# The first two weight units of a two-layer encoder: loaded and split in halves from a second queue, their products interleaved

## The chip, the cores and the metric

The kernel runs on one NeuronCore of one Trainium2 chip. The metric is device time in microseconds for one execution, the median over several runs. Everything (activations, both layers' attention, a dense feed-forward and a routed one with eight experts) is one launch.

## The reference

The input x is 512 rows of 1024 numbers in float32. Two layers follow each other; what concerns the change is the first step of the first one.

```python
h = rmsnorm(x, norm_mix[layer])      # x * rsqrt(mean(x*x)) * gain
...
proj = h @ w_in                      # 1024 x 4352: keys, queries, values, gates
...
merged = gates[:, :, 0] * (ya @ w_branch_a) + gates[:, :, 1] * (yb @ w_branch_b)
x = x + merged @ w_out
...
x = x + swiglu(...)  # layer 0;  x = x + moe_swiglu(...)  # layer 1, top 2 of 8 experts
```

## The kernel before

**Number format.** [...] A product is three matmuls: high weights by high activations, high weights by low activations, low weights by high activations.

**Units.** Weights come in units of 128 x 1024 floats (512 KB): eight tiles of 128 x 128, that is, 128 columns of a weight matrix over all 1024 rows of its input. `raw` holds four units as they land, `w_hi` and `w_lo` two split ones. For each unit ScalarE writes `w_hi` (L796, `split_hi`), VectorE writes `w_lo` (L1139, `split_lo`), TensorE makes 8 x 3 matmuls of 128x512, and it adds one to `unit_done`. Since there are two split buffers, ScalarE's split of unit n waits for `unit_done` to reach n - 1: the split of unit 2 waits for the products of unit 0.

**The input and its norm.** `xs` holds x transposed, in eight tiles k of 128 x 512 (256 KB each). ScalarE multiplies a tile by the gain and writes its high part `h_hi` (L849), VectorE the low part `h_lo` (L1164). The norm's factor is not known yet: the products of the first units run on the unscaled h, and the results are multiplied by `rms_inv` when they are evicted (L1178). Meanwhile ScalarE squares the tiles of x (L806) and VectorE adds them into `norm` (L1156, L1159). TensorE sums over the partitions (`mean_square`, L1686), ScalarE takes the root (L814), VectorE the reciprocal (L1169), which it places on a diagonal (L1173), TensorE spreads it over the partitions (`spread_rinv`, L1692), and ScalarE copies it out (`rms_inv`, L854).

**Queues.** All engines run their own list in program order; the order of the work is written by hand.
- SyncE issues the loads: gains, x0, unit 0, x1, unit 1, x2 to x7, units 2 and 3, and small tensors. A later unit n waits for `lo_ready` to reach n - 3.
- ScalarE: a warm-up of the root (its table load), x0, unit 0, x1, unit 1, x2 to x7, squares of x0 and x1, the split of unit 2 (behind the wait for unit 0's products), six more squares, the split of unit 3, the root, `rms_inv`. It issues no DMA.
- VectorE follows it with the low parts and the sums, in the same order.
- TensorE: 13 matmuls on an idle tile (`keep_warm`, L1662), then the 16 tile products of units 0 and 1 (`first_product`, L1736, L1738, L1741) in the order of `FIRST_PRODUCTS`: of unit 0 two tiles, of unit 1 two, then the six others of unit 0, then the six others of unit 1. Then unit 2 (`unit_ready` is a wait for its low part) with the mean before its sixth tile, unit 3 with the spread after its first tile, and unit after unit from there.

The matmuls of units 2 and up are L1655 to L1657.

Of the kernel before, what the change touches and what calls it, by code (L numbers as in the profile page):

```python
# [5 lines left out]
F32 = mybir.dt.float32  # L6
# [4 lines left out]
ALU = mybir.AluOpType  # L11
# [5 lines left out]
T = 512  # L17
# [51 lines left out]
def build_kernel(nc, xT, g_mix, w_in, b_gate, rel_ext, sinks, w_a, w_b, w_out, g_ffn, w_gu, w_down, w_router,  # L69
                 moe_gu, moe_down, g_ffn_row, g_final_row, out):  # L70
    ctx = ExitStack()
    with ctx:
# [3 lines left out]
        def sem(name):  # L76
            return ctx.enter_context(nc.semaphore(name))
# [189 lines left out]
        y0_done = sem("y0_done")  # L267
        last_rows_ready, last_hi, last_lo, placed, kept = (sem(n) for n in ("last_rows_ready", "last_hi", "last_lo", "placed", "kept"))
# [131 lines left out]
        def term(m, which):  # L400
# [7 lines left out]
        FIRST_PRODUCTS = ((0, 0), (0, 1), (1, 0), (1, 1), (0, 2), (0, 3), (0, 4), (0, 5), (0, 6), (0, 7),  # L408
                          (1, 2), (1, 3), (1, 4), (1, 5), (1, 6), (1, 7))
# [19 lines left out]
        def _(sp):  # L429
# [15 lines left out]

            sp.dma_start(gains[:, 0:DEPTH, :], g_mix).then_inc(gains_in, 16)
            load_x(0)
            load(0, w_in[0, 0])
            load_x(1)
            load(1, w_in[0, 1])  # L450
            for k in range(2, KD):
                load_x(k)
# [336 lines left out]
        def _(act_):  # L789
# [65 lines left out]

            A.wait_ge(basics, 1)
            warm_root()
            for k in range(2):
                h_split_hi(k)
                split_hi(k)  # L860
            for k in range(2, KD):
                h_split_hi(k)
# [272 lines left out]
        def _(V):  # L1135
# [54 lines left out]
            for k in range(2):  # L1190
                h_split_lo(k)
                split_lo(k)
            for k in range(2, KD):
                h_split_lo(k)
# [453 lines left out]
        def _(E):  # L1648
# [81 lines left out]
            def first_product(u, k):  # L1730

                (wh, wl), bank = split_of(u, k * P, (k + 1) * P), unit_bank(u)
                if k == 0:
                    E.wait_ge(hi_ready, u + 1)
                E.wait_ge(h_hi_ready, k + 1)
                E.matmul(ps[:, bank, :], wh, h_hi[:, k, :], start=k == 0, stop=False)  # L1736
                E.wait_ge(h_lo_ready, k + 1)
                E.matmul(ps[:, bank, :], wh, h_lo[:, k, :], start=False, stop=False)  # L1738
                if k == 0:
                    E.wait_ge(lo_ready, u + 1)  # L1740
                mm = E.matmul(ps[:, bank, :], wl, h_hi[:, k, :], start=False, stop=k == KD - 1)  # L1741
                if k == KD - 1:
                    mm.then_inc(unit_done, 1)

            E.wait_ge(basics, 3)
            keep_warm(13)
# [405 lines left out]
```

## Time and profile before

| | us |
|---|---|
| median of 3 runs | 1596.53 |
| lowest, highest | 1594.66, 1598.08 |
| the profiled execution's own time | 1595.05 |
| its span, from the first to the last instruction | 1593.2 |
| TensorE busy in it | 1572.4 |
| VectorE busy | 1012.4 |
| ScalarE busy | 842.6 |

Times in the rows below count from the start of the span. The opening, from the first instruction to unit 5, is the first 46 us. A row of the timeline gives a start and a length, and in brackets how long the engine had been idle before it and what it waited for. Lengths of matmuls are modelled; from one start to the next is the measured pace.

### The profile page before, as it was taken

Reading aid. Unit: us, or ns where it says so; the run is one execution under the profiler, and the core shown is the slowest. Engines: PE = TensorE matmul, PEld = TensorE weight load, DVE = VectorE, ACT = ScalarE, POOL = GpSimd, SP = SyncE. Lnnn points to the kernel's source line nnn. Section 1 sums busy time; section 2 is a strip of 40 time slices with the busy share of each in tenths; the row PEclk is TensorE's granted clock in tenths of the full one; section 3 lists DMA queues with packets and bytes.
Section 4 is the critical chain, followed back from the end, with each engine's and each line's share of the span. In section 5 each row is a group of like instructions: output and inputs, shape, how many; then the busy total and the mean of one; then the engine's idle time right before and its main releaser. Section 6 shows DMA issues by size and latency. Waiting matters only on the chain.

```text
span 1593.2 us, 22686 instructions
## 1 busy us (share of the span) xinstructions
PE 1572.4 (99%) x7620; PEld 1312.9 (82%) x7621; DVE 1012.4 (64%) x1699; ACT 842.6 (53%) x1321; POOL 236.7 (15%) x290
## 2 busy tenths in 40 slices
PE   9999999999999999999999999999999999999997
PEld 6788888788888888888888887778888888888886
DVE  6657765654444443346567666666666998887577
ACT  5436764343232332234357663566666888885564
POOL 0204563000000000002015660010101001110000
PEclk9999999999999999999999999999999999999999
DMA  7632222344454333335422123448767999996673
GB/s 221 193 100 68 68 64 70 96 142 137 141 149 129 93 91 100 91 103 149 114 70 78 54 67 93 159 164 292 242 221 242 376 382 376 382 373 216 205 245 131
DMA packets 90067, 266.37 MB, mean 167 GB/s; under 512 B 12594, under 2 KB 22834, under 8 KB 89969
## 3 DMA queue, kind: packets, MB, share of 16 engines
q1 hardware_dynamic: 82864, 248.59, 47.6%
q0 software_dynamic: 7104, 16.52, 3.3%
q8 instruction: 55, 0.90, 0.2%
q14 instruction: 44, 0.35, 0.1%
HBM read 243.63 MB, written 20.22 MB: 166 GB/s over the span
## 4 chain that ended last, share of the span: by engine, by line
PE 93%; DVE 4%; DMA 1%; issue 1%; ACT 1%; SPq 0%; POOL 0%; DVEq 0%; ACTq 0%; POOLq 0%
PE ps L1655 18%; PE ps L1656 17%; PE ps L1657 17%; PE ps L1992 8%; PE ps L1994 8%; PE ps L1993 8%; PE ps L1991 4%; PE ps L1990 4%; PE ps L1826 2%; PE ps L1859 1%; PE ps L1839 1%; PE ps L1858 1%; PE ps L1838 1%; PE ps L2001 1%; DVE w_lo L1139 1%; PE ps L1973 1%
## 5 line engine op out<-in xcount | busy, mean ns | idle before, releaser
L1655 PE MATMUL ps<-h_hi,w_hi 128*128 128x512 f32 x880 | 350.8, 399 | 1.6 <-DVE w_lo L1139 1.6
L796 ACT ACTIVATE w_hi<-raw 128x1024 fp32r<-128x1024 f32 (+1 forms) x168 | 175.9, 1047 | 327.1 <-PE ps L1657 323.7
L1656 PE MATMUL ps<-h_lo,w_hi 128*128 128x512 f32 x880 | 343.7, 391 | 0.0
L1657 PE MATMUL ps<-h_hi,w_lo 128*128 128x512 f32 x880 | 343.5, 390 | 0.0
L1139 DVE TENSOR_TENSOR w_lo<-raw,w_hi 128x1024 fp32r<-128x1024 f32 x136 | 164.4, 1209 | 136.2 <-ACT w_hi L796 136.0
L1144 DVE TENSOR_TENSOR m_lo<-m_raw,m_hi 128x1024 fp32r<-128x1024 f32 x144 | 168.4, 1192 | 68.9 <-ACT m_hi L836 61.0
L1657 PEld LDWEIGHTS ps<-h_hi,w_lo 128*128 128x128 f32 x880 | 165.2, 188 | 35.7
L1655 PEld LDWEIGHTS ps<-h_hi,w_hi 128*128 128x128 f32 x880 | 165.6, 188 | 27.7 <-issue 2.7
L1656 PEld LDWEIGHTS ps<-h_lo,w_hi 128*128 128x128 f32 x880 | 165.9, 189 | 25.5 <-issue 0.7
L836 ACT ACTIVATE m_hi<-m_raw 128x1024 fp32r<-128x1024 f32 x144 | 145.9, 1032 | 62.0 <-PE ps L1991 49.3
L1992 PE MATMUL ps<-m_hi,xt_hi 128*128 128x512 f32 (+1 forms) x320 | 120.3, 376 | 0.6 <-DVE xt_both L1148 0.6
L1144 DVE TENSOR_TENSOR m_lo<-h_rows,m_hi 128x1024 fp32r<-128x1024 f32 (+1 forms) x96 | 102.0, 1087 | 29.1 <-ACT m_hi L836 29.1
L1994 PE MATMUL ps<-m_hi,xt_lo 128*128 128x512 f32 (+1 forms) x320 | 119.4, 373 | 0.0
L1993 PE MATMUL ps<-m_lo,xt_hi 128*128 128x512 f32 (+1 forms) x320 | 119.3, 373 | 0.0
L836 ACT ACTIVATE m_hi<-h_rows 128x1024 fp32r<-128x1024 f32 (+1 forms) x96 | 90.1, 950 | 51.1 <-PE ps L1991 39.2
L595 POOL TENSOR_TENSOR w_lo<-raw,w_hi 128x512 fp32r<-128x512 f32 x64 | 82.5, 1291 | 52.0 <-DVE probs L1274 51.1
L607 POOL DMA_DIRECT2D norm<-rel_rows x16 | 9.7, 604 | 540.1 <-issue 465.7
L723 POOL DMA_INDIRECT xg<-h_dram,lists x18 | 24.1, 1337 | 372.7 <-PE ps L1973 296.1
L919 ACT ACTIVATE pT_hi<-ps 128x256 fp32r<-128x256 f32 (+3 forms) x128 | 50.5, 395 | 40.1 <-PE ps L1826 36.8
L1992 PEld LDWEIGHTS ps<-m_hi,xt_hi 128*128 128x128 f32 x320 | 60.1, 188 | 10.2 <-issue 0.8
L1655 PE MATMUL ps<-a_hi,w_hi 128*128 128x512 f32 x176 | 68.5, 389 | 0.0
L1656 PE MATMUL ps<-a_lo,w_hi 128*128 128x512 f32 x176 | 68.5, 389 | 0.0
(304 smaller groups left out, 3210.9 us busy)
## 6 DMA issues: line engine op xcount, KB each, us to landing
m_raw<-moe_g SPq DMA_DIRECT2D x88, 512.0 KB, 5.3
raw<-w_in SPq DMA_DIRECT2D x68, 512.0 KB, 3.6
m_raw<-moe_down SPq DMA_DIRECT2D x56, 512.0 KB, 6.1
raw<-w_gu SPq DMA_DIRECT2D x44, 512.0 KB, 3.7
h_rows<-moe_g SPq DMA_DIRECT2D x32, 512.0 KB
h_rows<-moe_g SPq DMA_DIRECT2D x32, 384.0 KB
h_rows<-moe_down SPq DMA_DIRECT2D x24, 512.0 KB
m_raw<-moe_g SPq DMA_DIRECT2D x24, 384.0 KB, 5.4
```

The costliest lines, as they stand in the source:

```text
L595: ins = pool.tensor_tensor(lo, raw[:, n % RAW, c0:c1], hi.bitcast(F32), ALU.subtract)
L796: A.activation(split_of(n, 0, cols)[0], raw[:, n % RAW, 0:cols], ACT.Copy).then_inc(hi_ready, 1)
L836: A.activation(hi_of(u)[:, 0:cols], raw_of(u)[:, 0:cols], ACT.Copy).then_inc(m_hi_ready, 1)
L1139: V.tensor_tensor(lo, raw[:, n % RAW, 0:cols], hi.bitcast(F32), ALU.subtract).then_inc(lo_ready, 1)
L1144: V.tensor_tensor(lo_part(u)[:, 0:cols], raw_of(u)[:, 0:cols], hi_of(u)[:, 0:cols].bitcast(F32), ALU.subtract).then_inc(m_lo_ready, 1)
L1655: E.matmul(ps[:, bank, :], wh, hi, start=first, stop=False)
L1656: E.matmul(ps[:, bank, :], wh, lo, start=False, stop=False)
L1657: return E.matmul(ps[:, bank, :], wl, hi, start=False, stop=final)
L1990: E.matmul(out, both[:, x, :], wh, start=start, stop=False)
L1992: E.matmul(out, hi[:, x, :], wh, start=start, stop=False)
L1993: E.matmul(out, hi[:, x, :], wl, start=False, stop=False)
L1994: return E.matmul(out, lo[:, x, :], wh, start=False, stop=stop)
```

## The change

**Loads.** The halves of units 0 and 1 (four tiles each, 256 KB) are loaded by four DMAs that ScalarE issues: the first halves of both before its table load, the second halves after the warm-up of the root. SyncE no longer loads units 0 and 1; it issues x0 first, then the gains, x1 to x7, units 2 and 3.

**Splits.** ScalarE and VectorE split units 0 and 1 in halves, in between the tiles of x. First halves have semaphores of their own (`early_raw`, `early_hi`, `early_lo`); the second halves use those of whole units.

**Products.** `FIRST_PRODUCTS` goes tile by tile: tile 0 of unit 0, tile 0 of unit 1, tile 1 of unit 0, and so on. TensorE waits for a half before tiles 0 and 4. The matmuls on the idle tile are 9 instead of 13.

```diff
--- before.py
+++ after.py
@@ -265,6 +265,7 @@
         rel_copied = [sem("rel_copied0"), sem("rel_copied1")]
         zero_sent, mix_open, premixed = sem("zero_sent"), sem("mix_open"), sem("premixed")
         y0_done = sem("y0_done")
+        early_raw, early_hi, early_lo = [sem("early_raw0"), sem("early_raw1")], sem("early_hi"), sem("early_lo")
         last_rows_ready, last_hi, last_lo, placed, kept = (sem(n) for n in ("last_rows_ready", "last_hi", "last_lo", "placed", "kept"))
         y_back = [sem(f"y_back{m}") for m in range(2 * TT)]
         mixed, mix_step, sq_ready, root_ready, inv_ready, scaled, act_out, dve_out = sem("mixed"), sem("mix_step"), sem("sq_ready"), sem("root_ready"), sem("inv_ready"), sem("scaled"), sem("act_out"), sem("dve_out")
@@ -405,8 +406,12 @@
 
         GATES_AT = {4 * g: g for g in range(N_GATE)}
 
-        FIRST_PRODUCTS = ((0, 0), (0, 1), (1, 0), (1, 1), (0, 2), (0, 3), (0, 4), (0, 5), (0, 6), (0, 7),
-                          (1, 2), (1, 3), (1, 4), (1, 5), (1, 6), (1, 7))
+        FIRST_PRODUCTS = [(u, k) for k in range(KD) for u in range(2)]
+        def first_half(n, half):
+            return slice(half * T, (half + 1) * T)
+
+        def split_half(n, half):
+            return split_of(n, half * T, (half + 1) * T)
 
         def halves(u):
 
@@ -443,12 +448,9 @@
             def load_x(k):
                 sp.dma_start(xs[:, k, :], xT[:, k, :]).then_inc(x_in[k], 16)
 
+            load_x(0)
             sp.dma_start(gains[:, 0:DEPTH, :], g_mix).then_inc(gains_in, 16)
-            load_x(0)
-            load(0, w_in[0, 0])
-            load_x(1)
-            load(1, w_in[0, 1])
-            for k in range(2, KD):
+            for k in range(1, KD):
                 load_x(k)
             load(2, w_in[0, 2])
             load(3, w_in[0, 3])
@@ -853,13 +855,32 @@
                 A.wait_ge(rinv_spread, j + 1)
                 A.activation(rms_inv[:], ps[:, SUM_BANK, :], ACT.Copy).then_inc(rms_ready, 1)
 
+            def load_half(n, half):
+                A.dma_start(raw[:, n, first_half(n, half)], w_in[0, n][:, first_half(n, half)]
+                            ).then_inc(raw_full[n] if half else early_raw[n], 16)
+
+            def split_hi_half(n, half):
+                A.wait_ge(raw_full[n] if half else early_raw[n], 16)
+                A.activation(split_half(n, half)[0], raw[:, n, first_half(n, half)], ACT.Copy).then_inc(hi_ready if half else early_hi, 1)
+
+            load_half(0, 0)
+            load_half(1, 0)
             A.wait_ge(basics, 1)
             warm_root()
-            for k in range(2):
-                h_split_hi(k)
-                split_hi(k)
-            for k in range(2, KD):
-                h_split_hi(k)
+            load_half(0, 1)
+            load_half(1, 1)
+            h_split_hi(0)
+            split_hi_half(0, 0)
+            h_split_hi(1)
+            split_hi_half(1, 0)
+            h_split_hi(2)
+            h_split_hi(3)
+            split_hi_half(0, 1)
+            h_split_hi(4)
+            split_hi_half(1, 1)
+            h_split_hi(5)
+            h_split_hi(6)
+            h_split_hi(7)
             square(0, 0)
             square(1, 1)
             split_hi(2)
@@ -1187,11 +1208,23 @@
                                        op1=ALU.max).then_inc(consts, 1)
                 V.wait_ge(consts, 3)
 
-            for k in range(2):
-                h_split_lo(k)
-                split_lo(k)
-            for k in range(2, KD):
-                h_split_lo(k)
+            def split_lo_half(n, half):
+                V.wait_ge(hi_ready if half else early_hi, n + 1)
+                hi, lo = split_half(n, half)
+                V.tensor_tensor(lo, raw[:, n, first_half(n, half)], hi.bitcast(F32), ALU.subtract).then_inc(lo_ready if half else early_lo, 1)
+
+            h_split_lo(0)
+            split_lo_half(0, 0)
+            h_split_lo(1)
+            split_lo_half(1, 0)
+            h_split_lo(2)
+            h_split_lo(3)
+            split_lo_half(0, 1)
+            h_split_lo(4)
+            split_lo_half(1, 1)
+            h_split_lo(5)
+            h_split_lo(6)
+            h_split_lo(7)
             sum_squares(0, 0)
             sum_squares(1, 1)
             split_lo(2)
@@ -1730,20 +1763,20 @@
             def first_product(u, k):
 
                 (wh, wl), bank = split_of(u, k * P, (k + 1) * P), unit_bank(u)
-                if k == 0:
-                    E.wait_ge(hi_ready, u + 1)
+                if k % 4 == 0:
+                    E.wait_ge(hi_ready if k else early_hi, u + 1)
                 E.wait_ge(h_hi_ready, k + 1)
                 E.matmul(ps[:, bank, :], wh, h_hi[:, k, :], start=k == 0, stop=False)
                 E.wait_ge(h_lo_ready, k + 1)
                 E.matmul(ps[:, bank, :], wh, h_lo[:, k, :], start=False, stop=False)
-                if k == 0:
-                    E.wait_ge(lo_ready, u + 1)
+                if k % 4 == 0:
+                    E.wait_ge(lo_ready if k else early_lo, u + 1)
                 mm = E.matmul(ps[:, bank, :], wl, h_hi[:, k, :], start=False, stop=k == KD - 1)
                 if k == KD - 1:
                     mm.then_inc(unit_done, 1)
 
             E.wait_ge(basics, 3)
-            keep_warm(13)
+            keep_warm(9)
             for layer in range(DEPTH):
                 n0 = MIX_START[layer]
                 norm_i = 2 * layer

```

What stands on ScalarE at its start before (`warm` is the warm-up of the root, `raw` and `w_hi` belong to weight units, `xs` and `h_hi` to the tiles of x):

```order
L810 ACT_TABLE_LOAD
L810 ACTIVATE warm<-eps 128x1 [waits basics]
L849 ACTIVATE h_hi<-xs,gains 128x512 [waits gains_in,x_in0]
L796 ACTIVATE w_hi<-raw 128x1024 [waits raw_full0]
L849 ACTIVATE h_hi<-xs,gains 128x512 [waits x_in1]
L796 ACTIVATE w_hi<-raw 128x1024 [waits raw_full1]
L849 ACTIVATE h_hi<-xs,gains 128x512 [waits x_in2]
L849 ACTIVATE h_hi<-xs,gains 128x512 [waits x_in3]
L849 ACTIVATE h_hi<-xs,gains 128x512 [waits x_in4]
```

and after the change:

```order
L859 DMA raw<-w_in 128x512 x2
L812 ACT_TABLE_LOAD
L812 ACTIVATE warm<-eps 128x1 [waits basics]
L859 DMA raw<-w_in 128x512 x2
L851 ACTIVATE h_hi<-xs,gains 128x512 [waits gains_in,x_in0]
L864 ACTIVATE w_hi<-raw 128x512 [waits early_raw0]
L851 ACTIVATE h_hi<-xs,gains 128x512 [waits x_in1]
L864 ACTIVATE w_hi<-raw 128x512 [waits early_raw1]
L851 ACTIVATE h_hi<-xs,gains 128x512 [waits x_in2]
L851 ACTIVATE h_hi<-xs,gains 128x512 [waits x_in3]
L864 ACTIVATE w_hi<-raw 128x512 [waits raw_full0]
L851 ACTIVATE h_hi<-xs,gains 128x512 [waits x_in4]
```

Four DMAs stand ahead of the first tile of x, and each split of a whole unit has become two of half its width, the second ones behind x3 and x4.

TensorE's first products before, where each group of three matmuls is a tile (the first two groups are unit 0, the third is unit 1):

```order
L1736 MATMUL ps<-h_hi,w_hi 128x512 [waits h_hi_ready,hi_ready]
L1738 MATMUL ps<-h_lo,w_hi 128x512 [waits h_lo_ready]
L1741 MATMUL ps<-h_hi,w_lo 128x512 [waits lo_ready]
L1736 MATMUL ps<-h_hi,w_hi 128x512 [waits h_hi_ready]
L1738 MATMUL ps<-h_lo,w_hi 128x512 [waits h_lo_ready]
L1741 MATMUL ps<-h_hi,w_lo 128x512
L1736 MATMUL ps<-h_hi,w_hi 128x512 [waits h_hi_ready,hi_ready]
L1738 MATMUL ps<-h_lo,w_hi 128x512 [waits h_lo_ready]
L1741 MATMUL ps<-h_hi,w_lo 128x512 [waits lo_ready]
```

and after the change (the first group is unit 0, the second unit 1, the third unit 0 again):

```order
L1769 MATMUL ps<-h_hi,w_hi 128x512 [waits h_hi_ready,early_hi]
L1771 MATMUL ps<-h_lo,w_hi 128x512 [waits h_lo_ready]
L1774 MATMUL ps<-h_hi,w_lo 128x512 [waits early_lo]
L1769 MATMUL ps<-h_hi,w_hi 128x512 [waits h_hi_ready,early_hi]
L1771 MATMUL ps<-h_lo,w_hi 128x512 [waits h_lo_ready]
L1774 MATMUL ps<-h_hi,w_lo 128x512 [waits early_lo]
L1769 MATMUL ps<-h_hi,w_hi 128x512 [waits h_hi_ready]
L1771 MATMUL ps<-h_lo,w_hi 128x512 [waits h_lo_ready]
L1774 MATMUL ps<-h_hi,w_lo 128x512
```

Unit 1's first tile has moved from the third to the second place, and the waits for a whole unit have become waits for its first half.

ScalarE again, behind the last tile of x, before (L806 are squares, L796 the splits of units 2 and 3):

```order
L806 ACTIVATE ps<-xs 128x512 [waits x_in0]
L806 ACTIVATE ps<-xs 128x512 [waits x_in1]
L796 ACTIVATE w_hi<-raw 128x1024 [waits unit_done,raw_full2]
L806 ACTIVATE ps<-xs 128x512 [waits summed,x_in2]
L806 ACTIVATE ps<-xs 128x512 [waits summed,x_in3]
L806 ACTIVATE ps<-xs 128x512 [waits summed,x_in4]
L806 ACTIVATE ps<-xs 128x512 [waits summed,x_in5]
```

and after:

```order
L808 ACTIVATE ps<-xs 128x512 [waits x_in0]
L808 ACTIVATE ps<-xs 128x512 [waits x_in1]
L798 ACTIVATE w_hi<-raw 128x1024 [waits unit_done,raw_full2]
L808 ACTIVATE ps<-xs 128x512 [waits summed,x_in2]
L808 ACTIVATE ps<-xs 128x512 [waits summed,x_in3]
L808 ACTIVATE ps<-xs 128x512 [waits summed,x_in4]
L808 ACTIVATE ps<-xs 128x512 [waits summed,x_in5]
```

Nothing moved here but the line numbers: the split of unit 2 waits for unit 0's products, and the squares of x2 to x7 stand behind it.

## Rows read from the trace of the kernel before

**Rows 1.** the page of the whole kernel, its parts 1 and 4

```profile
PE 1572.4 (99%) x7620; PEld 1312.9 (82%) x7621; DVE 1012.4 (64%) x1699; ACT 842.6 (53%) x1321; POOL 236.7 (15%) x290
...
PE 93%; DVE 4%; DMA 1%; issue 1%; ACT 1%; SPq 0%; POOL 0%; DVEq 0%; ACTq 0%; POOLq 0%
```

**Rows 2.** stretches: length, busy us (instructions) of each engine, PEclk, DMA share, GB/s

```profile
0.00:7.00 7.00, 5.21 (x13) 1.82 (x14) 0.77 (x2) 3.24 (x6) 2.32 (x15) 1.00 0.64 211
7.00:12.00 5.00, 3.94 (x15) 2.11 (x14) 4.27 (x5) 3.95 (x7) 0.00 (x0) 1.00 1.02 351
```

**Rows 3.** who waited for whom, first 60 us: us in total, times, longest

```profile
PE ps L1741 <- DVE w_lo L1139: 1.1, 2, 0.5
```

**Rows 4.** timeline from 0: start us, us, engine, line, operation, tiles, count, [idle <-releaser]

```profile
0.83 1.28 ACT L810 ACT_TABLE_LOAD   x1 [0.68 <-PEq L2144]
...
0.83 0.39 SPq L446 DMA_DIRECT2D gains<-g_mix  x1
...
1.27 0.43 SPq L444 DMA_DIRECT2D xs<-xT  x1
...
1.79 5.43 PE L1662 MATMUL ps<-idle 128*128 128x512 bf16 x13 [1.79 <-POOL ident L560]
...
2.12 0.20 ACT L810 ACTIVATE warm<-eps 128x1 f32<-128x1 f32 x1
...
39.93 0.57 POOL L580 DMA_DIRECT2D k_hi<-k_hi  x1 [0.38 <-POOL norm L613]
```

**Rows 5.** timeline near 1053 us, TensorE

```profile
1053.34 1.24 PE L1662 MATMUL ps<-idle 128*128 128x512 bf16 x5
```

**Rows 6.** timeline, ScalarE and VectorE, 4 to 14 us

```profile
4.47 0.72 ACT L849 ACTIVATE h_hi<-xs,gains 128x512 fp32r<-128x512 f32 x1 [2.15 <-DMA xs<-xT]
...
5.23 0.75 DVE L1164 SCALAR_TENSOR_TENSOR h_lo<-xs,gains,h_hi 128x512 fp32r<-128x512 f32 x1 [5.09 <-ACT h_hi L849]
...
5.98 1.06 ACT L796 ACTIVATE w_hi<-raw 128x1024 fp32r<-128x1024 f32 x1 [0.79 <-DMA raw<-w_in]
...
8.53 1.06 ACT L796 ACTIVATE w_hi<-raw 128x1024 fp32r<-128x1024 f32 x1 [0.88 <-DMA raw<-w_in]
...
11.60 2.03 ACT L849 ACTIVATE h_hi<-xs,gains 128x512 fp32r<-128x512 f32 x3 [0.17 <-DMA xs<-xT]
```

**Rows 7.** timeline, TensorE's first products, 7 to 16 us

```profile
7.09 0.50 PE L1736 MATMUL ps<-h_hi,w_hi 128*128 128x512 f32 x1
...
10.91 0.50 PE L1741 MATMUL ps<-h_hi,w_lo 128*128 128x512 f32 x1 [0.53 <-DVE w_lo L1139]
...
11.24 0.40 PE L1736 MATMUL ps<-h_hi,w_hi 128*128 128x512 f32 x1
...
15.79 0.39 PE L1741 MATMUL ps<-h_hi,w_lo 128*128 128x512 f32 x1
```

**Rows 8.** timeline, three engines, 13 to 29 us

```profile
16.28 1.06 ACT L796 ACTIVATE w_hi<-raw 128x1024 fp32r<-128x1024 f32 x1 [1.64 <-PE ps L1741]
...
17.37 1.23 DVE L1139 TENSOR_TENSOR w_lo<-raw,w_hi 128x1024 fp32r<-128x1024 f32 x1 [1.15 <-ACT w_hi L796]
...
18.52 4.64 DVE L1159 TENSOR_TENSOR norm<-norm,ps 128x512 f32<-128x512 f32 x6
...
20.10 0.39 PE L1655 MATMUL ps<-h_hi,w_hi 128*128 128x512 f32 x1
...
23.50 0.95 PE L1686 MATMUL ps<-mean_of,norm 128*128 128x1 f32 x8
...
24.99 0.69 DVE L1173 TENSOR_TENSOR norm<-ident,rinv 128x512 f32<-128x512 f32 x1
...
27.12 1.02 PE L1692 MATMUL ps<-norm,ones 128*128 128x512 f32 x2
28.18 0.60 ACT L854 ACTIVATE rms_inv<-ps 128x512 f32<-128x512 f32 x1 [3.43 <-PE ps L1692]
```

**Rows 9.** timeline, TensorE, its only start after an idle time in 40 to 46 us

```profile
45.38 0.47 PE L1655 MATMUL ps<-h_hi,w_hi 128*128 128x512 f32 x1 [1.56 <-DVE w_lo L1139]
```

## The prediction

> **What bounds the kernel now.** I read the page first. TensorE is busy for 1572.4 of 1593.2 us and makes 93% of the chain that ended last [rows 1], so time comes and goes only where TensorE is held up. The change touches the opening alone, so the next view is the list of waits there. TensorE waited 1.1 us for the low halves of the first two units (L1741) [rows 3], and ScalarE 1.64 us, before it splits unit 2, for TensorE to finish unit 0 [rows 8]. That second wait becomes the important one.
>
> Then the timeline. The first product starts at 7.09; the products run without a break only from the third product of unit 1's first tile, at 10.91 (10.91 to 11.24 is 0.33, a start after an idle time), and from 11.24 to 15.79 twenty starts lie 4.55 us apart, so **0.2275 us per product** [rows 7]. The 48 first products end, and unit 2 begins, at 20.10 [rows 8]. By then three other things have happened: unit 0's last product started at 15.79 [rows 7], ScalarE split unit 2 from 16.28, VectorE took the low half at 17.37 (1.23 us) and then added six squares in 4.64 us, until 23.16 [rows 8]. TensorE reached the mean (L1686) at 23.50, only 0.34 us after the last addition. So two chains run nearly side by side from 16.28 to 23.50: TensorE's products, and ScalarE and VectorE behind the end of **unit 0**. Behind the mean come VectorE's diagonal (24.99 to 25.68), TensorE's spread of the root in program order (27.12), and the evictions that wait for it (28.18) [rows 8]. The evictions pace what follows, for at 45.38 TensorE has stood still 1.56 us for VectorE's w_lo [rows 9]; after that I found no tie to absolute time. A shift of the mean therefore moves the rest of the kernel by as much.
>
> **The opening, step by step.** In blocks of 256 KB (a tile of x, or half a unit), the old queue delivers its 1st at 4.47, 3rd at 5.98, 6th at 8.53 and 10th at 11.60 [rows 6]: some 0.75 to 0.85 us a block. The first x tile is now issued at 0.83 instead of 1.27, as the gains change places with it [rows 4]: 0.44 us earlier. If x0 and unit 0's first half share the engines evenly, both are there when two blocks are, (4.47 + 5.98)/2 - 0.44 = 4.8; x1 and unit 1's first half at 5.98 + 0.85 - 0.44 = 6.4; x2 and unit 0's second half at 8.1; x3 and unit 1's second half (8th block, 8.53 + 1.54 - 0.44) at 9.6; x5 at 11.2. The total to x7 is the same twelve blocks. Without sharing x0 would land at 4.47 - 0.44 = 4.03; that is the lower end. The trace of before has one queue only, so the even share is my choice, on the ground that the DMA engines were full from 7 us on, at 351 GB/s [rows 2], and the bytes are the same. The Trainium skill (DMA: Bandwidth & Descriptors, section Issuing engines are not separate DMA queues) says that transfers started by different engines run on the same 16 DMA engines and interleave, so that the second queue saves issue time and gains no bandwidth; by that rule x0 comes at 4.8 rather than at 4.03, and the sum below is nearer to its +1.5 than to its lower end of +0.7. No run shown yet tells.
>
> ScalarE now issues four DMAs. No DMA of ScalarE is in the trace: SyncE takes 0.39 to 0.43, GpSimd 0.57 [rows 4]. With 0.45 each, two DMAs, the table load of 1.28 and two DMAs end at 0.83 + 0.9 + 1.28 + 0.2 + 0.9 = 4.1 (0.2 for the warm root [rows 4]); at 0.57 each it is 4.6. Either ends before x0 is there, so I cost them at nothing; the cover is 0.2 to 0.7 us.
>
> ScalarE's split of a tile of x takes 0.7 (0.72; three take 2.03), and VectorE's 0.75 [rows 6]. A split of half a unit I take as 0.6 on ScalarE (0.60 for the copy of rms_inv, of that size, and 1.06 for a whole unit) and 0.65 on VectorE (1.23 a whole one) [rows 6, 8]. So ScalarE: x0 4.8 to 5.5, unit 0's half to 6.1, x1 6.4 to 7.1, unit 1's half 7.15 to 7.75. VectorE: x0 5.5 to 6.25, unit 0's half to 6.9, x1 7.15 to 7.9, unit 1's half 7.9 to **8.55**. Product (0, 0) can start at 6.1, and the third product of (1, 0), number 6 of 48, at 8.6. From there all is ready in time: VectorE ends x2 at 9.6, x3 at 11.1, x4 at 12.5, unit 1's second half at 13.15 and x7 near 15.5, while pairs of tiles take 6 x 0.2275 = 1.36 us and the fifth starts at 8.95 + 3 x 1.36 = 13.0, its use of unit 1's half at 14.1, and the last pair at 17.1. The first products end at 8.95 + 42 x 0.2275 = **18.5, which is 1.6 us earlier** than 20.10. Nine warm-ups instead of thirteen (5.43/13 = 0.42 us each [rows 4]) end near 5.6, before the 6.1 at which TensorE is first wanted, and cost nothing by themselves.
>
> **What takes it back.** Unit 0 now ends three products before unit 1, not eighteen. Its last is number 45, at 8.95 + 38 x 0.2275 = 17.6. Before, 0.49 us lay between that product's start and ScalarE's split of unit 2 (15.79 to 16.28), so the split starts at 18.05, **1.77 us later** than before. Everything in that row of the queue follows: low half of unit 2 at 18.05 + 1.09 + 1.23 = 20.4 (TensorE idles 1.9 us after 18.5), last sum at 23.16 + 1.77 = 24.93. TensorE comes to the mean 15 products later, at 20.4 + 3.4 = 23.8, waits over 1 us more, and starts it at 25.0. The shift is 1.77 - 0.34 + 0.05 = **+1.5 us**. ScalarE's other work behind that wait (six squares, the split of unit 3) moves with it; unit 3, whose low half follows the last sum by 0.1 + 1.23, is ready at 26.3, and is wanted at 25.0 + 0.95 + 9 x 0.2275 = 28.0. The spread comes at 27.12 + 1.5, the evictions too, and the start at 45.38 becomes 46.9. The loads of units 2 and 3 and the later ones keep their order and have microseconds to spare.
>
> The profiled execution took 1595.05 (span 1593.2 and 1.85 around it), the median of the three runs is 1596.53. Sum: 1595.05 + 1.5 = 1596.55 against the profiled one, and **1598.0** against the median. Bounds of the sum: with the landings of unit 1 at 5.98 and ScalarE's splits of half of 1.06, number 6 starts at 7.8 and the shift is +0.7; with half a microsecond on each of the two landings it waits for, it starts at 9.6, the shift +2.5.
>
> **Rivals.** (a) *The clock comes up late: slower.* The thirteen warm-ups took 0.42 us each, five later ones 1.24/5 = 0.25 [rows 4, 5]: at first the clock is at its lower level, 1.2 GHz, though the column of granted clock reads 1.00 there [rows 2], and TensorE had worked without a break since 1.79 when it rose. Now the unbroken stretch ends at 5.6, with gaps up to 6.1, 6.9, 7.8 and 8.6. If the clock is still low at 8.6, and stays so as long as the warm-ups ran at it here, the products up to 14.0 run at 0.42 and lose 5.4 x (1 - 0.2275/0.42) = 2.5 us: 1.5 + 2.5 = +4.0, 1600.5. It decides if the first products start over 0.34 us apart. For it speaks the shorter warm-up; against, that TensorE is still at work for over half of 5.6 to 8.6. The Trainium skill (TensorE: Matmul & The Clock Gate, section What's actually happening) says that the throttled state is the default and activity releases it; the rows agree, but don't show what the gaps do.
> (b) *ScalarE's issues are slow, or its transfers late: slower.* At 1.2 us each instead of 0.45 its first split starts at 7.1, 2.3 late, and the shift is +3.8, 1600.3. Against it stand the rows of the two other engines.
> (c) *The 1.6 us are kept.* If unit 2 and the sums of squares were in time, 1596.53 - 1.6 = 1594.9. This needs ScalarE not to be held by unit 0; its queue has unit 2's split behind that very wait, before six of eight squares, so I give it little.
> (d) *The change does nothing:* products as late as before (20.10) through landings 1.6 us later than mine give the late split without the gain: +3.1, 1599.6.
>
> **Numbers.** 0.2% is 3.2 us, about what a measurement of this kernel tells from no change. The forecast (+0.7 to +2.5) has 0.66, (a) 0.15, (b) 0.06, (c) 0.06, (d) 0.07. Slower by over 3.2 us: (a), (b), and a part of (d) and of the forecast with scatter: 0.22. Faster by as much: 0.03, for only scatter beyond (c) gets there. The same: 0.75. Range: 1596.53 + 0.7 less the 1.9 by which the lowest run lies below the median gives 1595.3; the top takes in (a) and (b) with half a microsecond, 1601.0.
>
> **What would show it.** Number 6 of the first products near 8.6 and their end near 18.5; ScalarE idle some 2.5 us or more before it splits unit 2 near 18.0; TensorE idle 1.9 us before unit 2 (on VectorE's w_lo) and 1.2 before the mean (on norm), neither of which is there now; the mean near 25.0, the spread near 28.6. Wrong it would be if the mean came before 23.5, if products up to 14 were 0.42 apart, or if the 1.5 us were taken up in a later wait.

## The result, and the profile after it

The changed kernel takes **1600.37 us** (median of 11 executions, 1598.55 to 1602.92) against 1596.16 us for the kernel before (11 executions, 1594.66 to 1598.47). The ratio is 1.0030, with a 95% interval of 1.0022 to 1.0038: about 4 us slower, and slower by more than 0.2%. The profiled execution took 1599.41 us, its span is 1597.7, 4.5 more than before. Some executions are slower than any profile here shows: seven of the 49 of kernels with the interleaved order have a mean granted clock of 0.994 and took 1601.1 to 1604.0 us, none of the 154 listed of kernels with the old order is below 0.995, and no trace shows where in them the clock was low.

The page, its parts 1 and 4, against [rows 1]:

```profile
span 1597.7 us, 22686 instructions
...
PE 1573.3 (98%) x7616; PEld 1313.8 (82%) x7617; DVE 1011.1 (63%) x1701; ACT 842.8 (53%) x1323; POOL 236.5 (15%) x290
...
PE 91%; DVE 5%; issue 2%; ACT 1%; DMA 1%; DVEq 0%; ACTq 0%; POOL 0%; SPq 0%; POOLq 0%
```

TensorE's busy time grew by 0.9 us only, and the span by 4.5: TensorE stands still more. The timeline shows where, first the issues of the opening (SPq is SyncE's queue, ACTq ScalarE's), then TensorE up to its thirteenth product, with VectorE's low half of unit 1 that the sixth waits for, against [rows 4, 7] (start us, us, engine, line, operation, tiles, count, idle time before it):

```profile
0.83 0.39 SPq L449 DMA_DIRECT2D xs<-xT  x1
0.83 0.90 ACTq L859 DMA_DIRECT2D raw<-w_in  x2
1.27 0.43 SPq L452 DMA_DIRECT2D gains<-g_mix  x1
...
1.83 0.87 ACTq L859 DMA_DIRECT2D raw<-w_in  x2
...
1.79 3.82 PE L1695 MATMUL ps<-idle 128*128 128x512 bf16 x9 [1.79 <-POOL ident L562]
...
6.97 0.51 PE L1769 MATMUL ps<-h_hi,w_hi 128*128 128x512 f32 x1 [1.37 <-ACT w_hi L864]
...
8.58 0.72 PE L1769 MATMUL ps<-h_hi,w_hi 128*128 128x512 f32 x1 [0.24 <-ACT w_hi L864]
8.71 0.69 DVE L1214 TENSOR_TENSOR w_lo<-raw,w_hi 128x512 fp32r<-128x512 f32 x1
9.10 0.63 PE L1771 MATMUL ps<-h_lo,w_hi 128*128 128x512 f32 x1
9.53 0.72 PE L1774 MATMUL ps<-h_hi,w_lo 128*128 128x512 f32 x1
10.04 0.63 PE L1769 MATMUL ps<-h_hi,w_hi 128*128 128x512 f32 x1
...
12.15 0.39 PE L1774 MATMUL ps<-h_hi,w_lo 128*128 128x512 f32 x1
12.38 0.40 PE L1769 MATMUL ps<-h_hi,w_hi 128*128 128x512 f32 x1
```

then the splits of the first two tiles of x, and the stretch behind unit 0, against [rows 6, 8, 9]:

```profile
5.68 0.72 ACT L851 ACTIVATE h_hi<-xs,gains 128x512 fp32r<-128x512 f32 x1 [2.42 <-DMA gains<-g_mix]
...
7.28 0.72 ACT L851 ACTIVATE h_hi<-xs,gains 128x512 fp32r<-128x512 f32 x1 [0.36 <-DMA xs<-xT]
...
19.67 0.39 PE L1774 MATMUL ps<-h_hi,w_lo 128*128 128x512 f32 x1
...
20.16 1.06 ACT L798 ACTIVATE w_hi<-raw 128x1024 fp32r<-128x1024 f32 x1 [5.17 <-PE ps L1774]
...
21.25 1.22 DVE L1160 TENSOR_TENSOR w_lo<-raw,w_hi 128x1024 fp32r<-128x1024 f32 x1 [4.71 <-ACT w_hi L798]
...
22.39 4.64 DVE L1180 TENSOR_TENSOR norm<-norm,ps 128x512 f32<-128x512 f32 x6
22.52 0.50 PE L1688 MATMUL ps<-h_hi,w_hi 128*128 128x512 f32 x1 [1.79 <-DVE w_lo L1160]
...
27.08 1.05 PE L1719 MATMUL ps<-mean_of,norm 128*128 128x1 f32 x8 [0.86 <-DVE norm L1180]
...
28.68 0.69 DVE L1194 TENSOR_TENSOR norm<-ident,rinv 128x512 f32<-128x512 f32 x1
...
30.84 1.02 PE L1725 MATMUL ps<-norm,ones 128*128 128x512 f32 x2
...
31.90 0.60 ACT L856 ACTIVATE rms_inv<-ps 128x512 f32<-128x512 f32 x1 [3.46 <-PE ps L1725]
...
49.09 0.47 PE L1688 MATMUL ps<-h_hi,w_hi 128*128 128x512 f32 x1 [1.55 <-DVE w_lo L1160]
```

Unit 0's last product starts at 19.67 instead of 15.79. ScalarE stood idle for 5.17 us before it could split unit 2 (1.64 before), at 20.16 instead of 16.28. Behind that, TensorE idles 1.79 us for unit 2's low half and 0.86 us for the sums, two waits that were not there. The mean starts at 27.08 (23.50), the copy of rms_inv at 31.90 (28.18): **3.72 us later**. TensorE's start after an idle time is at 49.09 (45.38), with the same 1.55 us of idle time before it, and nothing takes the shift up for 1000 us: the five matmuls on the idle tile that stood at 1053.34 [rows 5] are at

```profile
1057.14 1.24 PE L1695 MATMUL ps<-idle 128*128 128x512 bf16 x5
```

3.80 us later. The issues of the last stores still start 3.7 us later (1588.38 against 1584.70, and 1589.96 against 1586.26). The remaining 0.8 us of the span arises in those stores and their landings; no run ties it to the change.

### The profile page after: what moved, and what is told of

The parts are those of the page before. It is cut to its first block, busy times and chain, and to the rows that moved or that the text cites. A ratio compares the mean times of both kernels' runs of the same rounds, so it can differ in the third digit from the quotient of the medians.

```text
span 1597.7 us, 22686 instructions
## 1 busy us (share of the span) xinstructions
PE 1573.3 (98%) x7616; PEld 1313.8 (82%) x7617; DVE 1011.1 (63%) x1701; ACT 842.8 (53%) x1323; POOL 236.5 (15%) x290
## 4 chain that ended last, share of the span: by engine, by line
PE 91%; DVE 5%; issue 2%; ACT 1%; DMA 1%; DVEq 0%; ACTq 0%; POOL 0%; SPq 0%; POOLq 0%
PE ps L1688 18%; PE ps L1689 17%; PE ps L1690 17%; PE ps L2025 7%; PE ps L2027 7%; PE ps L2026 7%; PE ps L2024 4%; PE ps L2023 4%; PE ps L1859 2%; PE ps L1892 1%; PE ps L1872 1%; PE ps L1891 1%; PE ps L1871 1%; PE ps L2034 1%; PE ps L2006 1%
## 5 line engine op out<-in xcount | busy, mean ns | idle before, releaser
L798 ACT ACTIVATE w_hi<-raw 128x1024 fp32r<-128x1024 f32 x166 | 173.8, 1047 | 328.9 <-PE ps L1690 323.6
L1160 DVE TENSOR_TENSOR w_lo<-raw,w_hi 128x1024 fp32r<-128x1024 f32 (+1 forms) x134 | 161.9, 1208 | 138.0 <-ACT w_hi L798 137.9
L1690 PE MATMUL ps<-a_hi,w_lo 128*128 128x512 f32 x176 | 68.5, 389 | 0.0
```

The lines of the kernel that those rows point to most:

```text
L798: A.activation(split_of(n, 0, cols)[0], raw[:, n % RAW, 0:cols], ACT.Copy).then_inc(hi_ready, 1)
L1160: V.tensor_tensor(lo, raw[:, n % RAW, 0:cols], hi.bitcast(F32), ALU.subtract).then_inc(lo_ready, 1)
L1690: return E.matmul(ps[:, bank, :], wl, hi, start=False, stop=final)
```

## The experiments

Each kernel computes all that the reference asks for. "Split" is the start of the split of unit 2, "copy" that of rms_inv, "restart" TensorE's start after its idle time near 45 us; ratios are to executions of the kernel before on the same chip.

| kernel | split | copy | restart | ratio, interval |
|---|---|---|---|---|
| before | 16.28 | 28.18 | 45.38 | 1 |
| the change | 20.16 | 31.90 | 49.09 | 1.0030, 1.0022 to 1.0038 |
| before, new order alone | 20.10 | 31.82 | 49.03 | 1.0041, 1.0027 to 1.0055 |
| change, old order | 16.13 | 28.02 | 45.21 | 1.0002, 0.9993 to 1.0012 |
| change, 13 warm-ups | 19.36 | 31.10 | 48.29 | 1.0027, 1.0016 to 1.0037 |
| change, gains first | 21.67 | 33.41 | 50.60 | 1.0039, 1.0025 to 1.0052 |
| change, squares first | 20.18 | 30.74 | 47.93 | 1.0023, 1.0013 to 1.0033 |
| change, one queue, 13 warm-ups | 18.79 | 30.54 | 47.73 | 1.0016, 1.0007 to 1.0025 |
| before, 9 warm-ups | 17.87 | 29.77 | 46.96 | 1.0002, 0.9993 to 1.0011 |
| before, mean sooner | 15.69 | 26.23 | 43.70 | 0.9992, 0.9983 to 1.0001 |
| the same again | 15.94 | 26.48 | 43.95 | 0.9994, 0.9986 to 1.0003 |
| change, mean sooner | 16.78 | 27.07 | 44.64 | 0.9999, 0.9990 to 1.0008 |
| before, mean sooner, x0 first | 16.28 | 26.82 | 44.28 | 0.9995, 0.9986 to 1.0004 |

In the first six rows, and wherever the order behind the split is untouched, the copy follows the split by 11.7 to 11.9 us: one number carries the whole opening. Split, copy and restart are of one profiled execution each; ratios whose intervals overlap don't tell two kernels apart.

### The order of the products alone

```diff
 # kernel before
-        FIRST_PRODUCTS = ((0, 0), (0, 1), (1, 0), (1, 1), (0, 2), (0, 3), (0, 4), (0, 5), (0, 6), (0, 7),
-                          (1, 2), (1, 3), (1, 4), (1, 5), (1, 6), (1, 7))
+        FIRST_PRODUCTS = [(u, k) for k in range(KD) for u in range(2)]
```

> The kernel before with the interleaved order of the first products and nothing else (whole loads, whole splits, 13 warm-ups). Theory (unit 0 ends late and holds the split of unit 2 and six squares): the sixth product stays near 10.9, unit 0's last product starts near 19.9 instead of 15.79, ScalarE splits unit 2 near 20.35, and the copy of rms_inv starts near 32.0 instead of 28.18; time +3.8 us against the kernel before. Rival (the order is harmless, the loss is in clock and landings): the copy stays within 0.7 us of 28.18, the time within 1 us.

The timeline of this kernel, ScalarE at unit 2 and TensorE behind it:

```profile
20.10 1.06 ACT L795 ACTIVATE w_hi<-raw 128x1024 fp32r<-128x1024 f32 x1 [5.75 <-PE ps L1740]
...
22.47 0.50 PE L1654 MATMUL ps<-h_hi,w_hi 128*128 128x512 f32 x1 [1.79 <-DVE w_lo L1138]
...
27.03 1.05 PE L1685 MATMUL ps<-mean_of,norm 128*128 128x1 f32 x8 [0.86 <-DVE norm L1158]
...
31.82 0.60 ACT L853 ACTIVATE rms_inv<-ps 128x512 f32<-128x512 f32 x1 [3.44 <-PE ps L1691]
```

The whole pattern of the change is there without its loads, its halves or its shorter warm-up: ScalarE's 5.75 us of idle time, TensorE's 1.79 and 0.86. The copy is 3.64 us late, where 3.8 were expected, and the time is up by 0.41%, 0.27% at the least. The rival is out. The 0.41% are 6.5 us, more than the copy explains: of only five executions two took 1603.08 and 1604.0 us; the medians are 4.5 us apart.

### The change with the old order

```diff
 # changed kernel
-        FIRST_PRODUCTS = [(u, k) for k in range(KD) for u in range(2)]
+        FIRST_PRODUCTS = ((0, 0), (0, 1), (1, 0), (1, 1), (0, 2), (0, 3), (0, 4), (0, 5), (0, 6), (0, 7),
+                          (1, 2), (1, 3), (1, 4), (1, 5), (1, 6), (1, 7))
```

> The changed kernel with the old order of the first products (unit 0 ends eighteen products before unit 1), halves and second queue kept. Theory: the split of unit 2 falls to 16 to 16.8 from 20.16, the copy of rms_inv to 28 to 28.6, time within 0.5 us of the kernel before although its loads are as in the change. Rival (halves and queue are what costs): the copy stays above 30 and the time 3 us or more above the kernel before.

```profile
1.79 4.02 PE L1696 MATMUL ps<-idle 128*128 128x512 bf16 x9 [1.79 <-POOL ident L563]
...
16.13 1.06 ACT L799 ACTIVATE w_hi<-raw 128x1024 fp32r<-128x1024 f32 x1 [1.30 <-PE ps L1775]
...
28.02 0.60 ACT L857 ACTIVATE rms_inv<-ps 128x512 f32<-128x512 f32 x1 [3.43 <-PE ps L1726]
```

Split at 16.13, copy at 28.02, ratio 1.0002. The two runs mirror each other: the order by itself gives the loss, and taking it back removes it with the loads, the halves and nine warm-ups all kept. What these bring or cost together is below what the ratio resolves (0.1% to either side, some 1.5 us).

### Thirteen warm-ups, and nine in the kernel before

```diff
 # changed kernel
-            keep_warm(9)
+            keep_warm(13)
```

```diff
 # kernel before
-            keep_warm(13)
+            keep_warm(9)
```

> The changed kernel with 13 warm-ups instead of 9. Theory (nine products between 8.6 and 12.1 ran 0.43 us apart because the clock fell): all first products 0.23 apart, the split of unit 2 near 18.9 instead of 20.16, the copy of rms_inv near 30.5 instead of 31.9, time 1.4 us below the changed kernel, still some 2.5 above the kernel before. Rival (the warm-ups don't matter): copy at 31.9, or later by the 0.2 us by which the warm-ups outlast the first split.

> The kernel before with 9 warm-ups instead of 13. Theory (the shorter warm-up costs only while products run low behind it, and in the order of before TensorE is waiting for loads until about 10.9 anyway): some first products 0.43 apart, the copy of rms_inv within 0.8 us of 28.2, time +0 to +1 us. Rival (the nine warm-ups are a large part of the change's 4 us): the copy at 29.5 or later, time +1.5 us or more.

First the stretch from 9 to 12.5 us in the changed kernel, then in the one with thirteen warm-ups (busy us and instructions of PE, PEld, DVE, ACT, POOL; then granted clock, DMA share, GB/s):

```profile
9.00:12.50 3.50, 3.50 (x10) 2.48 (x10) 3.02 (x6) 3.38 (x6) 0.00 (x0) 0.56 1.03 366
```

```profile
9.00:12.50 3.50, 3.34 (x13) 2.48 (x14) 3.41 (x6) 3.33 (x6) 0.00 (x0) 1.00 1.05 367
```

In the profiled execution of the change the granted clock was 0.56 in this stretch: for most of it at the lower level, 1.2 GHz. It had been up before: the first two products start 0.35 apart (6.97, 7.32), and the granted clock reads 1.00 from 7 to 8 us, 0.84 from 8 to 9 and 0.50 from 9 to 12; before it fell TensorE had stood idle for 1.37 and 0.24 us. The starts are 0.43 apart from 9.10 to 11.75 (but for one of 0.51) and 0.23 from 12.15 on. With thirteen warm-ups the granted clock is 1.00 and 13 products start, not 10. The split came at 19.36 instead of 20.16, 0.8 us sooner although x1 was split 0.45 us later (7.73 against 7.28). So the slow products behind the short warm-up cost this execution over a microsecond. The copy came at 31.10, not at the 30.5 expected, because x1 was late. The times don't show the 1.4 us that were expected: 1.0027 against 1.0030, with intervals that overlap.

The other kernel shows the same in the old order. Its profile has nine warm-ups and then every first product up to 13.94 at the slow pace; the next starts 0.25 later:

```profile
7.39 0.79 PE L1736 MATMUL ps<-h_hi,w_hi 128*128 128x512 f32 x1 [1.58 <-ACT w_hi L796]
7.99 0.63 PE L1738 MATMUL ps<-h_lo,w_hi 128*128 128x512 f32 x1
...
12.23 0.63 PE L1738 MATMUL ps<-h_lo,w_hi 128*128 128x512 f32 x1
12.66 0.63 PE L1741 MATMUL ps<-h_hi,w_lo 128*128 128x512 f32 x1
...
17.87 1.06 ACT L796 ACTIVATE w_hi<-raw 128x1024 fp32r<-128x1024 f32 x1 [3.34 <-PE ps L1741]
...
29.77 0.60 ACT L854 ACTIVATE rms_inv<-ps 128x512 f32<-128x512 f32 x1 [3.43 <-PE ps L1692]
```

There the copy is 1.6 us late, as the rival had it, yet the ratio over eleven executions is 1.0002. Its interval, 0.9993 to 1.0011, is -1.1 to +1.8 us and leaves room for both, so the runs don't decide between them. When the clock rises differs from one execution to the next: with identical code up to there, thirteen warm-ups took 5.43 us before, 5.73 with the new order alone and 4.48 with the mean sooner. The five profiles with nine warm-ups all have products 0.43 apart behind them, up to 10.6 us (change, old order) at the least and to 13.9 at the most; in none of the eight with thirteen does the slow pace last beyond 8 us. A profile gives the price of the slow pace in one execution; that most executions pay less of it would fit the times, but isn't shown.

### The gains, and one queue instead of two

```diff
 # changed kernel, SyncE: gains first
-            load_x(0)
             sp.dma_start(gains[:, 0:DEPTH, :], g_mix).then_inc(gains_in, 16)
-            for k in range(1, KD):
+            for k in range(KD):
                 load_x(k)
```

```diff
 # changed kernel with 13 warm-ups: SyncE issues the half units, ScalarE none
             load_x(0)
             sp.dma_start(gains[:, 0:DEPTH, :], g_mix).then_inc(gains_in, 16)
-            for k in range(1, KD):
-                load_x(k)
+            load_half(0, 0)
+            load_x(1)
+            load_half(1, 0)
+            load_x(2)
+            load_x(3)
+            load_half(0, 1)
+            load_x(4)
+            load_half(1, 1)
+            for k in range(5, KD):
+                load_x(k)
```

> The changed kernel with the gains issued before x0 again. Theory (x0's split waited for the gains, which landed behind x0 and the half unit): x0's split starts at 4.8 to 5.1 instead of 5.68, the first product near 6.3 instead of 6.97; the mean and the copy of rms_inv gain 0.5 to 0.9 us if the clock stays up and less if it falls. Rival (the landing of x0 itself is late because two queues share the engines): x0's split still at 5.5 or later.

> The change with 13 warm-ups and with its half units issued by SyncE between the tiles of x (x0, gains, unit 0's half, x1, unit 1's half, x2, x3, half, x4, half, x5 to x7), none by ScalarE. Theory (two queues share the engines, so x0 and x1 land late): x0's split starts at 4.0 to 4.6 instead of 5.7, x1's before 6.5 instead of 7.3 to 7.7, and the sixth product starts near 8.5 instead of 9.9; the copy of rms_inv 1 us or more before that of the two-queue kernel with 13 warm-ups (31.10). Rival (one queue delivers as late, the second is harmless): x0 at 5 or later, the copy within 0.4 us of 31.1.

Where the split of x0 had waited for the gains (5.68), with the gains first it waits for x0 itself, and with one queue it starts at 3.85; the kernels in this order:

```profile
5.61 0.72 ACT L850 ACTIVATE h_hi<-xs,gains 128x512 fp32r<-128x512 f32 x1 [2.35 <-DMA xs<-xT]
```

```profile
3.85 0.72 ACT L863 ACTIVATE h_hi<-xs,gains 128x512 fp32r<-128x512 f32 x1 [1.52 <-DMA gains<-g_mix]
...
6.64 0.72 ACT L863 ACTIVATE h_hi<-xs,gains 128x512 fp32r<-128x512 f32 x1 [0.78 <-DMA xs<-xT]
...
8.61 0.51 PE L1773 MATMUL ps<-h_hi,w_hi 128*128 128x512 f32 x1 [0.28 <-ACT w_hi L872]
```

The times from issue to landing take this apart. In the change x0, issued at 0.83, landed 4.2 us later, at 5.0; the gains, issued behind it at 1.27, landed at 5.6 and held the split. With the gains first these landed at 2.9, but x0, now issued at 1.27, took 4.3 us and landed at 5.6 too: the rival's number, and nothing won. With one queue x0, issued at 0.83 again, took 2.7 us and landed at 3.5, the gains at 3.8. The other kernels agree: with x0 first it took 3.5 to 4.3 us beside the half units of ScalarE's queue (four kernels) and 2.7 or 2.8 without (two). From one queue the split starts at 3.85, below the 4.03 that I had given as the lower end, and x1's at 6.64 instead of 7.28 to 7.73. The sixth product starts at 9.33 instead of 9.89, not at the 8.5 expected, because unit 1's half is split at 7.92 only. The copy comes 0.56 us sooner than with two queues (30.54 against 31.10), between theory (1 or more) and rival (0.4); the ratios, 1.0016 and 1.0027, have intervals that overlap. By the Trainium skill (DMA: Bandwidth & Descriptors, section Issuing engines are not separate DMA queues) both queues run on the same engines and interleave; x0's 4.2 us to its landing against 2.7 agree with that. What doesn't fit a plain reading is that the one-queue kernel moved less from 5 to 9 us, 265 GB/s:

```profile
5.00:9.00 4.00, 3.72 (x11) 1.76 (x9) 2.21 (x4) 2.30 (x4) 0.00 (x0) 1.00 0.84 265
```

against 385 in the change and 354 in the kernel before (the row of the same stretch). One execution each; I leave the cause open.

The kernel with the gains first also had the latest split of all, 21.67, and its copy came 1.5 us later than the change's where 0.5 to 0.9 sooner had been expected. Most of that is x1: it landed at 8.5 instead of 7.2, was split at 8.54, and the sixth product started at 10.85 instead of 9.53. The products ran 0.43 apart up to 13.86, which adds 0.2 us to what the change lost to the clock. That the order of the gains delays x1 isn't shown: the last kernel of the changed loads below has the gains first as well, and splits x1 at 7.50.

### The squares ahead of the split

```diff
 # changed kernel, ScalarE; VectorE likewise
-            split_hi(2)
             for k in range(2, KD):
                 square(k, k)
+            split_hi(2)
```

> The changed kernel with all eight squares (ScalarE) and their sums (VectorE) ahead of the split of unit 2, which still waits for unit 0. Theory (the shift has two parts, the late low half of unit 2 and behind it the late sums): TensorE's idle time before unit 2 stays near 1.8 us, the wait of 0.86 us before the mean is gone, so the copy of rms_inv comes 0.9 us nearer to ScalarE's split of unit 2 (10.8 us after its start instead of 11.74), and the time falls by 0.9. Rival (the sums don't matter, the split alone does): the distance stays 11.7.

```profile
22.53 0.50 PE L1688 MATMUL ps<-h_hi,w_hi 128*128 128x512 f32 x1 [2.22 <-DVE w_lo L1160]
...
26.06 0.95 PE L1719 MATMUL ps<-mean_of,norm 128*128 128x1 f32 x8
...
30.74 0.60 ACT L856 ACTIVATE rms_inv<-ps 128x512 f32<-128x512 f32 x1 [3.43 <-PE ps L1725]
```

The idle time before the mean is gone, as said, and the copy follows the split by 10.56 us instead of 11.74 (10.8 expected). TensorE's idle time before unit 2 has grown to 2.22 us, for another reason: here unit 0's last product starts at 19.24, but ScalarE is busy with its last square (from 19.64, 0.60 us), so the squares and no longer unit 0 hold the split, by some 0.45 us. Both parts of the loss are thus seen apart in the profile: about 1 us by the sums, the rest by unit 2's split. The time forecast, 0.9 us less than the change, is neither shown nor refuted: 1.0023 against 1.0030, with intervals that overlap.

### A version that doesn't lose: the mean sooner

In the kernel before ScalarE idled 1.64 us before the split of unit 2, TensorE did the mean only before its sixth tile, and the spread only behind unit 3's first. This edit uses all three, in the kernel before and, with the old order, 13 warm-ups and the gains first, in the change:

```diff
+            square(2, 2)              # ScalarE; VectorE: sum_squares(2, 2)
             split_hi(2)
-            for k in range(2, KD):
+            for k in range(3, KD):
...
-                        if k == 5:     # TensorE, unit 2
+                        if k == 4:
                             mean_square(0)
+                        if k == 7:
+                            spread_rinv(0)
...
-                        if k == 1:     # TensorE, unit 3
-                            spread_rinv(0)
```

> The kernel before, with the square and the sum of x2 ahead of the split of unit 2, the mean before tile 4 of unit 2 (was 5), and the spread before its tile 7 (was behind the first tile of unit 3). Theory (the evictions behind the spread pace TensorE up to 45 us): the copy of rms_inv starts near 26.9 instead of 28.2 and the start after idle at 45.4 moves to 44.1; time 1.3 us below the kernel before. Rival (TensorE's own products pace it): the copy is earlier, the start at 45.4 is not, time unchanged.

> The change with the old order of the products, 13 warm-ups, the gains before x0, and the same earlier mean and spread as in the kernel beside it. Theory: the split of unit 2 near 15.9 to 16.5, the copy of rms_inv near 26.6, time 1.6 us below the kernel before and some 6 below the changed one. Rival (as there): no better than the kernel before.

```profile
26.23 0.60 ACT L854 ACTIVATE rms_inv<-ps 128x512 f32<-128x512 f32 x1 [2.75 <-PE ps L1694]
...
43.70 0.47 PE L1657 MATMUL ps<-h_hi,w_hi 128*128 128x512 f32 x1 [0.47 <-DVE w_lo L1140]
```

The copy is at 26.23, 1.95 us sooner, and TensorE's idle time before its restart has shrunk from 1.56 to 0.47 us, the restart being 1.68 us sooner. The evictions did pace it. Of both shifts 0.59 us are not the edit's: the split of unit 2 itself came sooner in this execution (15.69 against 16.28), with the same code ahead of unit 0's end. The edit's own part is the distance from split to copy, 10.54 us instead of 11.90. The ratio is 0.9992 and its interval just reaches 1, so the kernel was run again, and a variant of it issues x0 ahead of the gains:

> The kernel before with the earlier mean and spread, once more and unchanged, to narrow an interval that just touched 1. Theory: the copy of rms_inv between 26 and 27, ratio to the kernel before 0.9990 to 0.9994, so that both sets of runs together lie below 1. Rival (the first set was luck): ratio 0.9998 or more.

> The kernel before with the earlier mean and spread (as in the kernel of that name) and with x0 issued ahead of the gains, still from one queue. Theory: the first split of x starts at 3.9 to 4.4 instead of 4.5 to 5.0, unit 1's low half 0.2 to 0.4 us sooner, the copy of rms_inv at 26.0, time 1.3 to 1.8 us below the kernel before and below the changed one by 5 to 6. Rival (the first products are paced by the later tiles of x, not by x0): the copy at 26.2 as without it, time as there.

0.9994 and 0.9995, each interval again reaching a little over 1. The first is inside what was expected. Three sets of eleven or twelve executions all lie below 1; the gain is likely 0.05% to 0.08%, about 1 us, and no single set shows it. Issuing x0 first had x0 split at 3.85, as expected, but unit 0 came later (split at 6.41 against 5.99) and the copy at 26.82, not at 26.0: nothing gained. In the changed loads the edit missed its forecast of 1.6 us below the kernel before: the ratio is 0.9999 (0.9990 to 1.0008), as the rival had it. Its split came at 16.78 and its copy at 27.07, not near 16.2 and 26.6, for TensorE had waited three times for the low part of a tile of x (0.28, 0.20 and 0.30 us). All four ratios lie 0.3% or more below the change's.

## Why the prediction was right, and where it was short

**The path.** The chain named was the one that decided: unit 0's end, ScalarE's split, the sums, the mean, the spread, the evictions. The rule of the sum (the mean and all behind it shift by what the split shifts, less 0.3) gives 20.16 - 16.57 = +3.6 for the changed kernel; measured are 3.58 at the mean and 3.72 at the copy. The two idle times were forecast as 1.9 and 1.2 us and are 1.79 and 0.86. The order alone, costed by the same rule from unit 1's low half of before, was expected at +3.8 and measured at +3.64. That no later wait takes the shift up also held: 3.80 at 1057 us, 3.7 at the last stores.

**The term that was mis-sized** is the start of that chain. The split of unit 2 was forecast at 18.05 and came at 20.16, 2.1 us later, so the shift was 3.7 and not 1.5 us, and the time 1600.4 and not 1598.0: inside the range, but beyond the upper bound of +2.5 that I gave the likeliest case, and slower by more than 0.2%, which had only 0.22. The range held only because its top had been drawn for rivals (a) and (b); that part is luck. Two steps of the sum make up the 2.1:

- *The landings, 0.85 us.* What decided was x1: forecast for 6.4, it landed at 7.2. ScalarE had waited 0.36 us for it, split it at 7.28, and unit 1's first low half ended at 9.40 and not 8.55. The sum shared the engines between two blocks at a time. But ScalarE issued the first halves of both units by 1.73, and the second halves from 1.83 on, beside its table load and not behind it (3.2 in the sum). By my estimate from the GB/s of the stretches, 5.8 blocks of 256 KB had been moved when x1 landed, where the count had four. The engines moved about as much as before (138 against 147 GB/s up to 5 us, 385 against 354 from 5 to 9), but a part of it was blocks that nobody was waiting for yet. No run takes the second halves away by themselves, so that they are what delayed x1 is argued and not shown. The first split started at 5.68 and not 4.8 for another reason: x0 itself landed at 5.0, 0.2 late, but the gains, which the change puts behind it and for which the sum had no term, at 5.6. ScalarE would still have been free for x1 at 6.92, so by this alone x1's split would have been about 0.5 us late.
- *The clock, 1.1 to 1.2 us.* From the sixth product at 9.53 the thirteenth should start at 9.53 + 0.33 + 6 x 0.2275 = 11.2 and did at 12.38. This is rival (a), at less than half its price of 2.5 us, since the clock was back by 12.15 and not 14.0; in two other profiles with nine warm-ups (the kernel before, the change with the gains first) the slow pace did last to 13.9. I had set forecast and rival apart as two cases, where some of the rival stands in all five profiles with nine warm-ups.

**The rivals.** (b), slow issues on ScalarE, is out: its four DMAs took 0.9 and 0.87 us a pair, as assumed, though late landings, which I had put under the same letter, did come, without a slow issue. (c), the gain kept, is out for the order of the change; with the old order the gain is 0.16 us in the copy, not 1.6. Its products ran 0.43 apart up to 10.61, and with 13 warm-ups (change, mean sooner) TensorE waited for the low parts of tiles of x. (d), late landings without the early start, is nearest in size: its +3.1 stands for products that end at 20.1, and here they end at 20.6. That it comes near is chance: in it all 1.6 us are landings, and here over half is the clock.

## What to carry to other kernels

Before interleaving the work of two buffers so that an engine starts sooner, ask when each buffer is released: if both are released at the end, whoever fills the next ones stands still, and the idle time saved at the front comes back behind, with all that waits in the same queue. Such a wait is best found on the queue of the engine that fills, by listing what stands behind it (here six squares and the mean's sums); if it must wait, put what doesn't depend on it in front. A transfer that is wanted first should have few others beside it: count every block that is in flight with it, and ask when a small transfer that the same work needs, like the gains, will land behind it. And before a filler that keeps TensorE at work is shortened, look at the distance of the starts behind it; what it cost here in the times is below what they resolve.

## What the runs showed of the chip that was not expected

- The time at which TensorE's clock rises in the opening differs between executions of the same instructions: thirteen warm-ups took 4.48, 5.43 or 5.73 us. The granted clock of the profile reads 1.00 even where the starts are 0.43 us apart (in the kernel with the gains first up to 13.86); the distance of the starts is the surer sign.
- A second queue delays the transfer that is needed first: x0, 256 KB issued at 0.83 us by SyncE, landed 3.5 to 4.3 us later with ScalarE's half units beside it (four kernels) and 2.7 or 2.8 us later without them (two kernels).
- ScalarE's queue issued DMAs (1.83 to 2.70) while its table load ran (1.76 to 3.04), though the program has them behind it.
